# Value projection from unnormalised x in an encoder step on one Trainium2 core

## What is computed

```python
h = rmsnorm(x, g_mix)                      # x * rsqrt(mean(x*x)+eps) * g_mix
z = h @ w_in                               # columns: pool u | q | k | v (512 each) | 8 forget logits
v = z[..., 1536:2048]; logf = log_sigmoid(z[..., 2048:] + b_f)
c_all = cumsum(concat([logf_hist, logf]))  # forget attention adds differences of c to its logits
...
x = x + concat([o_pool, o_fox]) @ w_o      # then memory attention, ConvFFN, final rmsnorm
```

## Time and profile before

| | us |
|---|---|
| time before, median of 3 runs | 946.47 (945.82 to 948.59) |
| profiled execution, own time | 950.01 |
| its span on the core | 948.2 |
| TensorE busy | 904.2 |
| VectorE busy | 521.3 |
| ScalarE busy | 357.8 |
| GpSimd busy | 54.2 |

### The profile page before, as it was taken

How to read it: one execution, slowest core, us unless ns; L and a number is a source line. 1 busy time by engine, 2 the same in 40 slices (tenths; PEclk the granted TensorE clock), 3 DMA queues, 4 the chain that set the end, 5 groups by cost and what they waited for, 6 DMA issues and landing times.

```text
span 948.2 us, 16526 instructions
## 1 busy us (share of the span) xinstructions
PE 904.2 (95%) x6402; PEld 866.0 (91%) x6402; DVE 521.3 (55%) x939; ACT 357.8 (38%) x574; POOL 54.2 (6%) x96
## 2 busy tenths in 40 slices
PE   4989999999899899998999999999999999999996
PEld 3878998999799679998999999999999999999996
DVE  4374675675576447554376665633466543356644
ACT  5253445543743445343234333221233321133323
POOL 4011101022100002000000000000000000000000
PEclk9997999999999999998999999999999999999998
DMA  6235332312622654220032223332222333232222
GB/s 196 67 100 152 94 89 76 84 37 88 197 84 87 213 205 139 75 66 23 23 88 89 78 77 88 88 89 69 86 72 83 88 89 87 69 88 69 69 84 101
DMA packets 116860, 88.89 MB, mean 94 GB/s; under 512 B 3168, under 2 KB 107830, under 8 KB 116819
## 3 DMA queue, kind: packets, MB, share of 16 engines
q1 hardware_dynamic: 111683, 71.15, 25.4%
q0 software_dynamic: 5136, 17.17, 6.0%
HBM read 81.32 MB, written 6.99 MB: 93 GB/s over the span
## 4 chain that ended last, share of the span: by engine, by line
PE 85%; DVE 5%; ACT 4%; DMA 3%; issue 2%; SPq 0%; DVEq 0%; ACTq 0%
PE ps L378 67%; PE ps L1688 3%; PE ps L1550 2%; PE ps L1886 2%; PE ps L1616 2%; DMA w_raw<-in_w_mk 2%; PE ps L1847 2%; ACT w_hi L389 1%; DVE w_lo L394 1%; PE ps L1659 1%; PE ps L1797 1%; PE ps L1617 1%; DVE y_tok L1514 1%; DMA x_tok<-in_x_prompt 1%; PE ps L1622 1%
## 5 line engine op out<-in xcount | busy, mean ns | idle before, releaser
L394 DVE TENSOR_TENSOR w_lo<-w_raw,w_hi 128x1024 fp32r<-128x1024 f32 x124 | 152.5, 1230 | 206.1 <-ACT w_hi L389 203.7
L378 PE MATMUL ps<-a_hi,w_hi 128*128 128x288 f32 x1024 | 223.8, 300 | 3.5 <-DVE w_lo L394 1.6
L378 PE MATMUL ps<-a_lo,w_hi 128*128 128x288 f32 x1024 | 220.8, 298 | 0.0
L378 PE MATMUL ps<-a_hi,w_lo 128*128 128x288 f32 x1024 | 220.7, 297 | 0.0
L389 ACT ACTIVATE w_hi<-w_raw 128x1024 fp32r<-128x1024 f32 x124 | 130.8, 1055 | 224.7 <-PE ps L378 184.5
L378 PEld LDWEIGHTS ps<-a_hi,w_hi 128*128 128x128 f32 x1024 | 166.3, 191 | 5.7 <-DVE w_lo L394 1.2
L378 PEld LDWEIGHTS ps<-a_hi,w_lo 128*128 128x128 f32 x1024 | 166.5, 190 | 0.0
L378 PEld LDWEIGHTS ps<-a_lo,w_hi 128*128 128x128 f32 x1024 | 166.5, 190 | 0.0
L378 PE MATMUL ps<-b_hi,w_hi 128*128 128x288 f32 x608 | 131.1, 297 | 2.3 <-DVE x_t L1351 1.5
L378 PE MATMUL ps<-b_lo,w_hi 128*128 128x288 f32 x608 | 130.0, 296 | 0.0
L378 PE MATMUL ps<-b_hi,w_lo 128*128 128x288 f32 x608 | 129.8, 295 | 0.0
(11 more groups left out here) (346 smaller groups left out, 1249.5 us busy)
## 6 DMA issues: line engine op xcount, KB each, us to landing
w_raw<-in_w_up SPq DMA_DIRECT2D x44, 512.0 KB, 3.8
w_raw<-in_w_in SPq DMA_DIRECT2D x16, 512.0 KB, 4.0
w_raw<-in_w_down SPq DMA_DIRECT2D x16, 512.0 KB, 3.7
w_raw<-in_w_o SPq DMA_DIRECT2D x8, 512.0 KB, 3.7
w_raw<-in_w_mk SPq DMA_DIRECT2D x8, 512.0 KB, 3.3
w_raw<-in_w_mv SPq DMA_DIRECT2D x8, 512.0 KB, 3.2
w_raw<-in_w_mq SPq DMA_DIRECT2D x8, 512.0 KB, 3.8
w_raw<-in_w_mo SPq DMA_DIRECT2D x8, 512.0 KB, 3.7
```

The costliest lines, as they stand in the source:

```text
L378: mm = nc.tensor.matmul(acc[:, h, 0:H], w[slot][:, c], x[:, k, h * H:h * H + H], start=(k == first and w is w_hi and x is x_hi), stop=(k = ...
L394: nc.vector.tensor_tensor(w_lo[slot][:], w_raw[slot][:], w_hi[slot][:].bitcast(F32), ALU.subtract).then_inc(weight_lo_ready, 1)
```

## The change

x is turned as it landed, and values are computed from x times g_mix alone; the rms factor of the token is applied when v is evicted. The gate, q, k and u still need the normalised x: it is made from a kept copy of the turned x, over the place of the value stage's input, while that stage runs. The kept copy is stored in DRAM and read back later in the turned layout, in place of the second load and turns of x. The start loads x before the sample and half a weight ahead. The first projection of q starts when two of four value tiles are free, k when all are.

Core of the diff, the order of loads first:

```diff
@@ sync
-            for t in (NT, 0, 1, 2, 3):
+            for t in range(NT + 1):
                 sp.dma_start(x_tok[0:x.shape[0], t, :], x).then_inc(x_landed[t], 16)
+                if t == NT - 1:
+                    sp.dma_start(w_raw[0][:, 0:DFOX], w_in[0:P, v_cols]).then_inc(weight_first_landed, 16)
+            sp.dma_start(w_raw[0][:, DFOX:2 * DFOX], w_in[P:2 * P, v_cols]).then_inc(weight_landed[0], 16)
+            sp.dma_start(w_raw[1]..., w_in[2 * P:4 * P, v_cols]...).then_inc(weight_landed[1], 16)
...
+                if j == 0:
+                    sp.wait_ge(x_kept, KT + 1)
+                    sp.dma_start(x_dram, x_keep[:].rearrange("p k t -> p (k t)")).then_inc(x_saved, 16)
...
-            sp.wait_ge(turn_done, len(TURNS))
-            sp.wait_ge(scores_done, N_ENTRIES)
-            sp.wait_ge(vc_ready, PAIRS)
-            sp.wait_ge(wp_landed, 16)
-            for t in range(NT):
-                sp.dma_start(x_again[:, t, :], ...).then_inc(misc_landed, 16)
-            sp.dma_start(x_again[0:TS, NT, :], a["x_sample"][0]).then_inc(misc_landed, 16)
+            sp.wait_ge(x_saved, 16)
+            sp.wait_ge(pv_done, N_ENTRIES)
+            sp.dma_start(x_t[:].rearrange("p k t -> p (k t)"), x_dram).then_inc(misc_landed, 16)
@@ gpsimd
+            pool.wait_ge(x_landed[NT - 1], 16)
             small(wf_raw[:], ...)
@@ scalar (in queue order; copy = a copy with a scale, rounding where the output is a high part)
+            squares_of(0); squares_of(1); squares_of(2)
+            turned_hi(0); copy(w_hi[0][:, 0:DFOX], ...); turned_hi(1); copy(w_hi[0][:, DFOX:2 * DFOX], ...)
+            copy(xs_both[:, :, 0:TS], x_gained_s[:]); copy(x_keep[:, :, TP:T], ...)
+            keep(0); keep(1); round_weights(act, 1, 1)
+            turned_hi(2); squares_of(3); keep(2); squares_of(NT)
+            nc.scalar.activation(stat[:, 8:8 + NT + 1], stat[:, 0:NT + 1], ACT.Sqrt, ...).then_inc(x_rms, 1)
+            turned_hi(3); round_weights(act, 2, 0); keep(3); turned_hi(4); keep(4)
+            normed_high(0); normed_high(1); turned_hi(5); round_weights(act, 3, 1); keep(5)
+            normed_high(2); normed_high(3); turned_hi(6); keep(6); ...
+            turned_hi(7); round_weights(act, 4, 0); keep(7)
+            normed_high(4); normed_high(5); normed_high(6); normed_high(7)
             for t in range(NT):
-                copy(v_hi[:, t, :], bank)
-                copy(v_out[:, t, :], bank).then_inc(v_copied, 1)
+                copy(v_hi[:, t, :], bank, scale)
+                copy(v_out[:, t, :], bank, scale).then_inc(v_copied, 1)
+                if t == 1:
+                    round_weights(act, 5, 1)
@@ vector (in queue order)
+            turned_lo(0); minus(w_lo[0][:, 0:DFOX], ...); turned_lo(1); (x_gained_s); minus(w_lo[0][:, DFOX:], ...)
+            minus(xs_both[:, :, TS:P], ...); rest_of_weights(dve, 1, 1); turned_lo(2); (masks, constants)
+            nc.vector.reciprocal(stat[:, 48:48 + NT + 1], ...).then_inc(x_scale, 1)
+            turned_lo(3); rest_of_weights(dve, 2, 0); (copy of the turned scales into inv_rms)
+            turned_lo(4); (copy of the sample's); normed_value(0); normed_value(1); normed_low(0); normed_value(2)
+            turned_lo(5); rest_of_weights(dve, 3, 1); normed_low(1); normed_value(3); normed_low(2)
+            normed_value(4); turned_lo(6); normed_low(3); normed_value(5); ...
+            turned_lo(7); rest_of_weights(dve, 4, 0)
+            for k in range(4, KT): normed_low(k); normed_value(k + 2) where there is one
             dve.wait_ge(weight_used, 4)
             (vs_sum twice)
+            value_low(0); value_low(1)
             dve.wait_ge(gate_done, 1)
             (z, z_min)
+            rest_of_weights(dve, 5, 1); value_low(2); value_low(3)
             (logf, both scans)
+            (own_lo)
@@ tensor
+            for t in range(NT):
+                pe.wait_ge(x_landed[t], 16)
+                (turn feature tiles 0 and 1 of this token tile)
+            pe.wait_ge(x_landed[NT], 16)
+            (8 turns of the sample, raw)
+            for k in range(KT):
+                values(k)                      # waits h_lo_ready k+1, weight_lo_ready as before
+                if k == 1: (turns of the constant rows, 7)
+                if k == 2: wait x_scale 1, cols_ready 4; scale_turn(0, NT, P)
+                if k + 2 < KT: h_turn(k + 2)   # waits x_kept k+2
+                if k == 2: wait scale_rows 1; scale_turn(NT, NT + 1, TS)
             (gate matmuls, each tile after normed_ready k+1)
-            pe.wait_ge(v_copied, NT + 1)
-            pe.wait_ge(v_free, NT + 1)
-            (8 turns of cl_tok; then q; then k)
+            pe.wait_ge(v_free, 2)
+            project(0, a_hi, a_lo, ACC[0], range(KT), KT)
+            pe.wait_ge(vs_ready, 1)
+            (8 turns of cl_tok)
+            pe.wait_ge(v_free, 4)
+            project(1, a_hi, a_lo, ACC[1], range(KT), KT)
...
-                for n in range(turned, min(turned + 2, len(MISCS))):
-                    misc_turn(n)
+                if i < 4:
+                    misc_turn(MEMORY_TURNS + i)
```

More of the change, by code:

```diff
@@ L206, in build @@
         cum_s = place("cum_s", [HEADS, KEYS])
-        assert here[0] <= at["wf_raw"]
+        wf_raw = place("wf_raw", [P, KT, HEADS])
+        wf_hi = place("wf_hi", [P, KT, P], F32R)
+        wf_both = place("wf_both", [P, KT, P], F32R)
+        cl_tok = place("cl_tok", [P, CT, HEADS])
+        rows_in = place("rows_in", [P, 3, P])
+        hist_tok = place("hist_tok", [16, DPOOL])
+        causal = place("causal", [P, P])
+        here[0] = at["b_hi"]
+        x_keep = place("x_keep", [P, KT, T])
+        assert here[0] <= at["b_lo"]
+        here[0] = at["b_lo"]
+        xs_both = place("xs_both", [P, KT, P], F32R)
+        vs_sum = place("vs_sum", [TS, DFOX])
+        normed = place("normed", [P, 2, T])
+        assert here[0] <= at["ident"]
         here[0] = phase
@@ new lines, in keep, with normed_high @@
+            def keep(k):
+                act.wait_ge(h_lo_ready, k + 1)
+                copy(x_keep[:, k, 0:TP], turn_bank(k)).then_inc(x_kept, 1)
+            def normed_high(k):
+                act.wait_ge(weight_used, k // 2 + 1)
+                act.wait_ge(normed_made, k + 1)
+                copy(a_hi[:, k, :], normed[:, k % 2, :]).then_inc(normed_hi, 1)
+            squares_of(0)
+            squares_of(1)
+            squares_of(2)
+            act.wait_ge(cols_ready, 1)
+            turned_hi(0)
@@ L1186, in _ @@
             nc.vector.tensor_tensor_scan(cum_s[:], ones_row[:], log_s[:], 0.0, mult, sub).then_inc(cum_ready, 1)
+            dve.wait_ge(v_copied, NT + 1)
+            scaled_minus(own_lo[:], vs_sum[:], stat[0:TS, 48 + NT:49 + NT], f32(own_hi[:])).then_inc(v_free, 1)
             def finish_q(j):
@@ new lines, in _ @@
+            ins.then_inc(hs_turned, 1)
+            for k in range(KT):
+                values(k)
+                if k == 1:
+                    pe.wait_ge(rows_landed, 16 * 4)
+                    pe.wait_ge(more_rows_landed, 16 * 4)
+                    pe.wait_ge(cols_ready, 1)
+                    turn(bank[:, 0:NG], rows_in[0:NG, 0, :], ident[0:NG, 0:NG])
+                    turn(bank[:, 64:64 + 4 * NF], rows_in[0:4 * NF, 1, :], ident[0:4 * NF, 0:4 * NF])
+                    turn(bank[:, 192:192 + 2 * NF], rows_in[0:2 * NF, 2, :], ident[0:2 * NF, 0:2 * NF])
+                    for g in range(GROUPS):
+                        ins = turn(bank[:, 256 + 16 * g:256 + 16 * g + NHIST], hist_tok[0:NHIST, g * P:g * P + P],
+                                   ident[0:NHIST, 0:NHIST])
+                    ins.then_inc(cols_turned, 1)
+                if k == 2:
+                    pe.wait_ge(x_scale, 1)
+                    pe.wait_ge(cols_ready, 4)
+                    scale_turn(0, NT, P)
@@ L1574, in _ @@
                 if k + 2 < KT:
                     h_turn(k + 2)
-                values(k)
+                if k == 2:
+                    pe.wait_ge(scale_rows, 1)
+                    scale_turn(NT, NT + 1, TS)
             pe.wait_ge(wf_ready, 1)
-            pe.wait_ge(cols_ready, 4)
-            pe.wait_ge(h_lo_ready, KT)
-            pe.wait_ge(sample_split, 1)
+            pe.wait_ge(scale_rows, 2)
+            pe.wait_ge(x_kept, KT + 1)
             for k in range(KT):
+                pe.wait_ge(normed_ready, k + 1)
@@ L1757, in _ @@
                 pool_map(n)
-                misc_turn(2 * n + 2)
-                misc_turn(2 * n + 3)
+                for m in range(2 * n + 2, min(2 * n + 4, MEMORY_TURNS)):
+                    misc_turn(m)
             def mean(n, value, bank):
```

265 lines of the change are left out of this document (153 added, 112 removed).

## The result

| | us |
|---|---|
| time after, median of 14 runs | 940.27 (938.34 to 946.29) |
| time before, median of 14 runs beside them | 946.48 (942.20 to 952.08) |
| ratio after to before | 0.9949, 95% interval 0.9926 to 0.9972 |
| profiled execution of after, own time | 938.85 (span 937.1) |
| forecast | 936.0 (930.0 to 942.0) |

Faster, as forecast, and inside the range. But the forecast gain was 10.5 us; the ratio makes it 4.8 (2.6 to 7.0), the two medians 6.2. The two profiled executions differ by 11.1 in span, which taken alone would seem to confirm the forecast. Both numbers need an explanation.

A forecast was written before the change was run, and what follows sets the result against it. TensorE, busy 95% of the 948.2 us span, was taken as the bound. Gains of 5.2 (start) and 5.3 (output stretch) sum to 10.5: 939.5 from the profiled 950.01, 936.0 from the median 946.47; range 930.0 to 942.0.

The forecast's parts named there:

- Values(0): First tile of the value stage: starts at 13.4 instead of about 18.0, 4.6 us earlier.
- Rival (d): Value stage: clock stays at 0.50, each tile costs 2.8 us more, five make 950.0; chance 0.07 with anything leaving no difference.
- (b): Value stage: VectorE's queue sets the pace, five tiles lose 0.7 us each, 939.5; chance 0.19 together with (c).
- (c): Late transfers: x at 11.4, w_pool behind the reload, 0.8 + 1.0 us, 941.3 with (b); chance 0.19 together with (b).
- I take 0: Output stretch: w_pool's load beside the reload of x delays its rounding and the pool chain by 0 us.
- bound 1: Output stretch: if w_pool lands behind all 2.25 MB, its rounding and the pool chain slip by up to 1 us.
- of 5 us slack 3.5 remain, so this costs nothing: Third score step: decay rows come only 3.7 us earlier, but 3.5 of 5 us slack remain, so no cost.
- Without that cover, 1.5: Third score step: price of 1.5 us if the slack does not cover the decay rows.
- The forecast keeps this: Attention's first steps: the low clock, 13 us at half speed costing up to 6.5, stays as in the profile before.
- the difference of 3.5 between profile and median: Whole kernel: profiled execution of before lies 3.5 us over its median; the same difference is taken after the change.
- Rival (a): Attention's first steps: the clock rises sooner or never falls, 4.5 or 6.5 us more gained, about 930.5; chance 0.14.
- 5.2 + 5.3: Gains summed to 10.5 us: first scores 5.2 earlier, output projection 5.3 earlier.

The follow-up runs named there:

- w_pool_first: Changed kernel with one more wait on SP: the reload of x waits until w_pool has landed; 938.92 us, ratio 0.9935 to the kernel before.
- before_warm: Kernel before with nine matmuls of 512 columns, result unread, in the wait ahead of the first scores; 943.94 us, ratio 0.9985.
- after_warm: Changed kernel with ten matmuls of 512 columns, result unread, in the wait ahead of the first scores; 945.54 us, ratio 0.9995 to the kernel before.
- decay_early: Changed kernel with turns and copy of cached forget values moved earlier and v's prompt part stored once evicted; 941.92 us, ratio 0.9949 to the kernel before.
- k_early_decay: w_pool_mem plus decay_early's edits and the first cached keys loaded ahead of the sums; 933.73 us, ratio 0.9861 to the kernel before.
- the filler: Unread matmuls of 512 columns in TensorE's wait ahead of the first scores, nine in the kernel before (before_warm); 943.94 us, ratio 0.9985.
- undo_reload: Changed kernel with the second load of x and its 40 turns put back, only the new start kept; 944.40 us, ratio 0.9976 to the kernel before.
- w_pool_mem: w_pool_first plus the first two memory turns moved ahead of the wait before the first output piece; 937.24 us, ratio 0.9922 to the kernel before.
- decay_w_pool: k_early_decay without the early load of the cached keys, so w_pool_mem with decay_early's edits; 936.79 us, ratio 0.9900 to the kernel before.
- after_again: The changed kernel once more, unaltered, for a second trace; 941.69 us, ratio 0.9961 to the kernel before.
- k_early: w_pool_mem with the first cached keys loaded right behind the store of v, ahead of the sums; 942.42 us, ratio 0.9955 to the kernel before.

## Why the prediction was right and wrong

**Right, by its own marks.** Values(0) at 13.1 (forecast 13.4). Values ending at 45.66 (45.2), in part by luck: all twelve matmuls of values(0) were slow (4.86 against 2.77, so 2.1 where the forecast took 1.0), and the sum counts a turn for each of eight tiles, where the last two have none, which is 0.9 too much. The wait behind the gate 0.86 (0.8), with the clock up behind it. First scores at 66.96 (66.5). The stores and the copy of x cost nothing, the output pieces alternate with memory turns alone, and the wait ahead of the first piece grew from 0.81 to 1.68 (1.7). Rival (d) did not happen. Nor did (b) at its price: TensorE waited 0.3 in the value stage, though the chain shows VectorE pacing what comes behind it. Of (c) w_pool came behind the reload, at twice the price given there, and the sample landed at 11.94 (3.57 + 8.37), near the forecast's 12.1. That was luck too: in the twelve executions with the new start its turns begin at 11.94 to 13.35, and only in three ahead of 12.1.

**Wrong: w_pool's load, "I take 0", bound 1.** It took 9.6 us and cost 2.0 in the profiled execution (22.7 instead of 20.7 to the first output piece). The bound was wrong too, since it rested on the whole 2.25 MB landing in 7 to 7.5 us, about the start's rate; the reload took 9.9. The row for it, 3.4 us, was of a load that was alone. The prediction set beside it the Trainium skill's rule (DMA: Bandwidth & Descriptors, Arbitration) that an engine takes turns between queues by packets, and took from it a slip of 0. The trace does not bear that reading out: the small load landed 0.1 us after the large one (221.37 + 9.9 and 221.80 + 9.6). w_pool_first shows that the reload is what held it up; how the engines share is not shown. The sign set for this, a low part of w_pool less than 5 us earlier, was too weak: it came 5.04 earlier (232.12 against 237.16) while the last weighted value came 7.7 earlier.

**Wrong: the decay rows, "of 5 us slack 3.5 remain, so this costs nothing".** The slack was the distance from 74.94 to the third step at 80.25, and TensorE was at half speed between them. In after the rows are taken at 71.98, which is 3.0 earlier and not 3.7, and the third step is at 74.34, so 2.4 were left, and only because the clock was low there. A slack read in a slow stretch shrinks when that stretch gets quick. before_warm has 77.14 - 75.28 = 1.9 left, of which the step from VectorE's row to TensorE's takes 0.35 (73.83 to 74.18 in after_warm), and the change moves TensorE by 5.1 and the decay rows by 1.45: 5.1 - 1.45 - 1.5 gives 2.2, and the wait in after_warm is 2.12. The same holds for the cached keys, which the text did not price. "Without that cover, 1.5" was on record, but as a price of the wait alone, and the wait can bring a fall of the clock that is dearer: decay_early against k_early_decay is 6.0 us in the attention of the two profiled executions, for a wait of 1.8 on the keys. In the timed runs this is a likely share of the shortfall and not a shown one.

**Wrong: the clock, "The forecast keeps this", and the difference of 3.5 between profile and median carried over.** The low stretch of 13.7 us in before is no fixed part of the kernel: its usual run has 13 us less at half speed than the profiled one, and the filler, which took 6.0 off the profiled attention, takes 1.4 off the timed runs, whose mean clock it leaves within 0.001. So the 3.5 was in the main this execution's clock (13 us at 0.3 each make 4), and nothing to carry over; after's profiled execution lies 1.4 below its median. Seen by the clock of the timed runs, the marks that the change moves (4.7 and 3.1, together 7.8) less 2 to 3.5 for the longer time at half speed give 4.3 to 5.8, around the measured 4.8. Seen by stages, against an execution of before without the low stretch, after's lead at the last weighted value is 71.67 + 151.4 - 221.30 = 1.8, not 7.7; undo_reload, timed in 12 runs, gives 2.3; with 3.1 for the output stretch that makes 4.9 to 5.4. That before's profile flattered the change is shown by the clocks on record. Which wait of after brings its longer time at half speed is not: the 1.68 ahead of the first output piece is a candidate, since the clock fell behind it in w_pool_first and after_warm, and w_pool_mem, where it is 0.81, has a mean of 0.986. Rival (a) saw that the clock could do better, and half of it came, the low stretch being 6.8 instead of 13.7; it did not see that before might do better by itself.

**The sum.** 5.2 + 5.3 was built against one execution with a long low stretch. What came of it in the profiles is 3.1 of the 5.3 (w_pool 2.0 lost, 0.2 on the small terms) and 4.7 of the 5.2. In the timed runs the start is worth about 2 (2.3 by undo_reload), most likely because the usual run of before is not as slow behind it as the profiled one.

## What to carry to other kernels

Before a slack is used as cover, look at the granted clock between the two times that make it, and work it out again for a quick TensorE. Before a profile is used as the base of a forecast, compare its mean clock with that of the timed runs. When a stage is pulled forward, list everything that did not move as far, small transfers and their place in a queue above all, for a wait there can cost the clock besides itself. And a small load that the next stage needs is issued ahead of a large one that has time, by a wait if need be.

## What was not expected of the hardware

- **The fall of the clock is not a function of the wait's length alone.** It fell behind TensorE waits of 1.69 (w_pool_first), 1.77 (decay_early), 2.12 (decay_w_pool, after_warm) and 2.31 (after), and not behind 1.68 (after), 1.82 (after) and 2.13 (k_early_decay). Equal waits had both outcomes.
- **A fall can cost more than the wait.** One of 10.2 us with TensorE busy costs about 5 (an estimate, half of it), behind a wait of under 2.
- **A quick TensorE can be the slower one.** after_warm removed a fall ahead of the attention, and its timed runs are 3 to 4 us slower than after_again's (3.2 by the ratios, whose intervals overlap slightly, 3.9 by the medians); its profile has three others in its place.
- **256 KB took 3.1 to 3.4 us alone and 9.6 beside 2.25 MB of another queue.** The decay rows took 5.2 us in k_early_decay and 8.6 in k_early, where v's store was issued 4.9 us ahead of the sums and not 9.6. The keys stood 3 to 3.6 us ahead of the sums in both.
